# Column-wise norm roots spread by transposes, a tile-stepped first pair, and unrolled layers in a two-layer streaming encoder

## The chip, the cores and the metric

The kernel runs on one core of a Trainium2 chip. The metric is the device time of one launch in microseconds (us); lower is better. The engines are TensorE (PE, with its weight loads shown apart as PEld), VectorE (DVE), ScalarE (ACT), GpSimd (POOL) and SyncE (SP, which here issues the weight transfers).

## What is computed

Two layers run over 544 tokens at once: 512 prompt tokens (no history) and 32 later tokens with 256 cached ones. Each layer is a half-step gated feed-forward block, a mixer of three attention branches, and a second half-step feed-forward block. Each of these is a sandwich of two norms:

```
def rmsnorm(x, g):  return x * rsqrt(mean(x*x, axis=-1) + 1e-6) * g      # over 1024 features

def ffn_half(x, pre_g, w_up, w_down, post_g):
    h = rmsnorm(x, pre_g)
    gate, up = split(h  w_up, 2)                    # 1024 -> 2 * 2816
    y = (silu(gate) * up)  w_down                   # 2816 -> 1024
    return x + 0.5 * rmsnorm(y, post_g)

def mixer(x, ...):
    u = rmsnorm(x, mix_pre_gain)                     # then u  w_in, three attentions, gates, w_o
    return x + rmsnorm(y, mix_post_gain), new_rows

for l in range(2):
    x = ffn_half(x, ..0..);  x, new = mixer(x, ..);  x = ffn_half(x, ..1..)
```

The outputs are x after the second layer and the new cache rows of both layers.

## The kernel before, in words

**Layout.** Activations lie feature-major: `xT` is 128 partitions by 8 feature tiles by 544 tokens. A norm's sum over features is therefore a sum over partitions and over eight tiles. Products run in a split form: every weight tile is rounded to a high part by ACT (`high`, line 1030, into `piece_h` in the feed-forward blocks and `piece_m` in the mixer) and the rest is taken by POOL (`low`, line 398, back into the weight ring). Inputs are split in the same way, `uT_r` high and `u_l` or `u_lm` low. `split_product` (lines 584 to 602) does, for each of 8 feature tiles, high weight by high and by low input, in two token halves of 272 columns (4 matmuls at line 595), and then in a second sweep low weight by high input (2 at line 600): 48 matmuls for one 128-wide output tile. A feed-forward pair is a gate tile in PSUM unit 0 (banks 0 and 1) and an up tile in unit 1 (banks 2 and 3).

**Norms.** There are six wide norms in a layer: `pre_a`, `post_a`, `mix`, `mix_post`, `pre_b`, `post_b`. Before a sub-layer, ACT squares each new tile of `xT` into one of two `sq` buffers and `square_sum` (line 568) multiplies it by a 128x128 matrix of ones, two full fp32 matmuls of 272 columns for each of 8 tiles, so that the sum arrives in every partition of banks 4 and 5. After a sub-layer DVE adds seven squared tiles (line 1390) and `sum_partitions` (lines 578 and 581) does the same with two such matmul pairs. Then ACT takes the root of 128x544 (line 1009) and DVE the reciprocal (line 1364). `post_norm` scales tile k (line 1402) and adds tile k-1 to `xT` (line 1398). In a feed-forward block the input is split before its root is known (ACT line 1043, DVE line 1417) and the root is applied to the gate and up products (lines 1427 and 1429); the DVE splits stand behind the whole of `post_norm` in its queue. In the mixer the input is scaled first (line 1377) and then split (1025, 1374).

**Order at a boundary.** PE runs the eight square sums, then the gate tile of the first pair (its first sweep waits for tile k of the input at each k), then the up tile. The next gate tile needs unit 0 back from DVE (line 1427) and a new high piece from ACT.

**Loops.** Every engine has a hardware loop over the two layers (`Fori(0, DEPTH)`), with shorter ones within the feed-forward blocks. Semaphore targets are computed in registers from the loop variable. Gains of the layer are copied into `g_now` (lines 1649 and 1655).

**Start.** A table of position biases is made by PE and ACT (lines 538, 997) in the place where `act_h` will lie. POOL writes it to memory (line 382) and waits until it has landed (line 383) before its first `low`. DVE waits for the same before the first gated tile (line 1440).

## Time and profile before

| | us |
|---|---|
| median of 3 runs (3488.01 to 3491.17) | 3488.42 |
| the profiled execution | 3489.38 |
| its span, first to last instruction | 3487.8 |
| PE busy, share of the span | 3297.6, 95% |
| PEld busy | 2965.1, 85% |
| DVE, ACT, POOL busy | 1476.1, 1032.8, 1064.5 |
| share of the chain that ended last | PE 90%, DVE 5% |

The table is read from the top: PE sets the time in nearly all stages, so what is left lies in the stretches in which it waits or runs at a lower clock. These are the start of the kernel and the boundaries between sub-layers. PE's durations are modelled, and a busy PE is not one that streams at its peak: the share of a stretch in which columns stream has to be worked out from its instructions. The granted clock of a stretch is 1.0 at 2.4 GHz and 0.50 at 1.2 GHz.

### The profile page before, as it was taken

How to read it: one execution, taken by the hardware profiler on the slowest of the kernel's cores; microseconds unless marked ns; L12 is line 12 of the kernel's file. 1: busy time of each engine (PE TensorE's matmuls, PEld its weight loads, DVE VectorE, ACT ScalarE, POOL GpSimd, SP SyncE). 2: the span in 40 equal slices, each digit the busy share in tenths (PEclk: the TensorE clock that was granted, in tenths of full speed). 3: DMA queues.
4: the chain of work that ended last, by engine and by line, in shares of the span. 5: the costliest groups of instructions: out<-in, count | busy, mean ns of one | idle time of the engine just before them, and what ended most of it. 6: DMA issues, size and time to landing. Idle time of an engine off the chain costs nothing.

```text
span 3487.8 us, 57668 instructions
## 1 busy us (share of the span) xinstructions
PE 3297.6 (95%) x23070; PEld 2965.1 (85%) x23070; DVE 1476.1 (42%) x1874; ACT 1032.8 (30%) x1686; POOL 1064.5 (31%) x499
## 2 busy tenths in 40 slices
PE   3999989999999998999989999899999999899997
PEld 3999976966678898999989999779467779899997
DVE  1555141841235545554265531358202354365533
ACT  2222223243223323222232222332622232232221
POOL 1344322310213242334323443323011213334342
PEclk7999987998999999999999999889989999999999
DMA  5221232210111131221212212312011112312223
GB/s 128 85 84 70 91 112 77 77 41 10 61 37 58 55 114 64 94 84 65 105 69 90 84 67 98 107 65 85 9 50 39 46 50 72 115 61 90 83 73 118
DMA packets 43712, 259.99 MB, mean 75 GB/s; under 512 B 6112, under 2 KB 6208, under 8 KB 26112
## 3 DMA queue, kind: packets, MB, share of 16 engines
q1 hardware_dynamic: 37584, 239.83, 19.4%
q0 software_dynamic: 5840, 17.50, 1.9%
q8 instruction: 122, 2.00, 0.2%
q14 instruction: 70, 0.57, 0.1%
q10 hardware_dynamic: 96, 0.08, 0.0%
HBM read 241.54 MB, written 15.85 MB: 74 GB/s over the span
## 4 chain that ended last, share of the span: by engine, by line
PE 90%; DVE 5%; issue 2%; another core or an unknown queue 2%; ACT 1%; DMA 0%; DVEq 0%; POOL 0%; ACTq 0%; POOLq 0%
PE PS L595 38%; PE PS L600 19%; PE PS L784 11%; PE PS L945 2%; PE PS L556 2%; PE PS L683 2%; PE PS L704 2%; PE PS L896 1%; PE PS L898 1%; PE PS L795 1%; PE PS L568 1%; PE PS L809 1%; PE PS L825 1%; PE PS L812 1%
## 5 line engine op out<-in xcount | busy, mean ns | idle before, releaser
L398 POOL TENSOR_TENSOR ring_r<-ring,piece_h 128x1024 fp32r<-128x1024 f32 (+1 forms) x240 | 628.8, 2621 | 1066.0 <-ACT piece_h L1030 1010.7
L398 POOL TENSOR_TENSOR ring_r<-ring,piece_m 128x1024 fp32r<-128x1024 f32 (+1 forms) x172 | 365.8, 2131 | 1008.5 <-ACT piece_m L1030 1008.2
L595 PE MATMUL PS<-u_l,piece_h 128*128 128x272 f32 x2816 | 581.6, 288 | 0.0
L595 PE MATMUL PS<-uT_r,piece_h 128*128 128x272 f32 x2816 | 580.4, 287 | 0.6 <-DVE u_l L1417 0.6
L1030 ACT ACTIVATE piece_h<-ring 128x1024 fp32r<-128x1024 f32 (+1 forms) x240 | 275.0, 1147 | 1023.1 <-PE PS L600 1022.8
L600 PE MATMUL PS<-uT_r,ring_r 128*128 128x272 f32 x3648 | 497.1, 288 | 40.7 <-POOL ring_r L398 40.7
L600 PEld LDWEIGHTS PS<-uT_r,ring_r 128*128 128x128 f32 x3648 | 474.4, 189 | 40.9 <-POOL ring_r L398 40.9
L595 PEld LDWEIGHTS PS<-uT_r,piece_h 128*128 128x128 f32 x2816 | 441.0, 188 | 2.3 <-DVE u_l L1417 1.0
L595 PEld LDWEIGHTS PS<-u_l,piece_h 128*128 128x128 f32 x2816 | 440.4, 188 | 0.0
L595 PE MATMUL PS<-act_h,piece_h 128*128 128x272 f32 x1408 | 291.5, 288 | 0.0
L595 PE MATMUL PS<-act_l,piece_h 128*128 128x272 f32 x1408 | 291.4, 289 | 0.0
L1030 ACT ACTIVATE piece_m<-ring 128x1024 fp32r<-128x1024 f32 (+1 forms) x172 | 160.7, 936 | 368.4 <-PE PS L600 268.5
L1390 DVE TENSOR_TENSOR rstd<-rstd,sq 128x544 f32<-128x544 f32 x36 | 103.8, 2884 | 361.8 <-ACT sq L1002 361.8
L1429 DVE TENSOR_TENSOR sq<-sq,rstd 128x544 f32<-128x544 f32 x88 | 192.7, 2190 | 132.0 <-ACT sq L1048 132.0
L595 PEld LDWEIGHTS PS<-act_l,piece_h 128*128 128x128 f32 x1408 | 220.8, 188 | 0.0
L595 PEld LDWEIGHTS PS<-act_h,piece_h 128*128 128x128 f32 x1408 | 220.5, 189 | 0.0
L1437 DVE TENSOR_TENSOR act_l<-sq,act_h 128x544 f32 x88 | 211.3, 2401 | 10.8
L595 PE MATMUL PS<-uT_r,piece_m 128*128 128x272 f32 x832 | 180.2, 299 | 14.0 <-DVE u_lm L1374 13.3
L600 PE MATMUL PS<-act_h,ring_r 128*128 128x272 f32 x1408 | 186.2, 287 | 0.0
L600 PEld LDWEIGHTS PS<-act_h,ring_r 128*128 128x128 f32 x1408 | 179.9, 188 | 0.0
L595 PE MATMUL PS<-u_lm,piece_m 128*128 128x272 f32 x832 | 177.1, 295 | 0.0
L784 PE MATMUL PS<-uT_r,piece_m 128*128 128x272 f32 x768 | 163.8, 295 | 1.1 <-DVE xT L1524 1.1
(229 smaller groups left out, 4760.3 us busy)
## 6 DMA issues: line engine op xcount, KB each, us to landing
ring<-in_w_up SPq DMA_DIRECT2D x92, 1024.0 KB, 4.7
ring<-in_w_dn SPq DMA_DIRECT2D x64, 704.0 KB, 4.1
ring<-in_w_mg SPq DMA_DIRECT2D x48, 768.0 KB, 4.2
ring<-in_w_in SPq DMA_DIRECT2D x24, 1024.0 KB, 4.8
ring<-in_w_out SPq DMA_DIRECT2D x8, 1024.0 KB, 4.8
x_spill<-xT SPq DMA_DIRECT2D x2, 2176.0 KB, 8.7
xT<-x_spill SPq DMA_DIRECT2D x2, 2176.0 KB, 8.6
ring<-in_w_vb SPq DMA_DIRECT2D x4, 1024.0 KB, 4.7
```

The source lines that it names most:

```text
L398: nc.gpsimd.tensor_tensor(ring_r[:, ch[0] % NSLOT, at:at + n], w, hi, ALU.subtract).then_inc(S["w_low"], 1)
L556: ins = mm(PS[0:m, 2 * u + b, 0:n[b + 1] - n[b]], w, x[:, n[b]:n[b + 1]], start=first and s == 0, stop=last and s == len(steps) - 1)
L595: mm(PS[:, 2 * u + b, 0:HALF], w, x[k][:, HALF * b:HALF * b + HALF], start=first and k == 0 and n == 0, stop=False)
L600: ins = mm(PS[:, 2 * u + b, 0:HALF], w_l[:, k * P:(k + 1) * P], x_h[k][:, HALF * b:HALF * b + HALF], start=False, stop=last and k == K - 1)
L683: ins = mm(PS[:, banks[s], :], tokens(x, k, s), w[:, n], start=k == 0 and m == 0, stop=k == KD - 1 and m == 2)
L704: mm(PS[:, 6 + i % 2, 0:w], qI[r:r + 64, h // 2, P * s:P * s + P], kI[r:r + 64, k0:k0 + w], start=True, stop=True).then_inc(S["idx_done"], 1)
L784: ins = mm(PS[:, 2 * u + j % 2, 0:HALF], w, x[:, k, half], start=j < 2, stop=j >= 6 * K - 2)
L945: ins = mm(out, pt, V[0:m, vt, hv:hv + DH], start=n == 0, stop=n == len(tiles) - 1)
L1030: A(buf[:, hs, 0:n], ring[:, ch % NSLOT, at:at + n], ACT.Copy).then_inc(S["w_high"], 1)
L1390: ins = V.tensor_tensor(rstd[:], rstd[:], sq[:, k % 2, :], ALU.add) if k else V.tensor_copy(rstd[:], sq[:, 0, :])
L1429: V.tensor_tensor(g, g, rstd[:], ALU.mult).then_inc(S["gate_step"], 1)
L1437: V.tensor_tensor(lo, g, hi.bitcast(F32), ALU.subtract).then_inc(vacated[1], 1)
```

## The change

1. **Sums by token.** For the wide norms, `token_sums` replaces `square_sum`: the squared tile is the stationary operand, in five blocks of 128 tokens, and one column of ones streams past. The result is one column for each block, 128 tokens in the partitions. The root and the reciprocal are taken of 128x5 (`wide_root`, `finish`).
2. **Spread.** DVE multiplies a matrix of ones by each of the five columns (128x128 each), and PE transposes the five, so that every partition has the row of all tokens again, now in PSUM banks 4 and 5 (`r_tok`). The scaling of `post_norm` and of the mixer's input reads it there. A feed-forward block copies it to `rstd` first.
3. **Steps by tile.** Where a feed-forward block follows, `post_norm` on DVE goes scale, split, add for each tile instead of splitting all tiles at the end. On PE, `first_pair` runs gate and up tile together by feature tile: 8 matmuls for tile k, then (in feed-forward blocks) the token sums of tile k, then the 4 low-weight matmuls of tile k-3. ACT makes the high input before the square. The mixer's first two tiles go the same way after all its sums.
4. **Layers unrolled.** The loops over the layers are Python loops; targets are constants; `g_now` is gone. The four weight loads that followed the last block are gone.
5. **Table.** It lies at another address, and the wait for its landing moves on POOL to where it is read back; DVE's wait is gone. ACT loads the silu table set ahead of the loop.

```diff
+WIDE = {"pre_a": 0, "post_a": 1, "mix": 2, "mix_post": 3, "pre_b": 4, "post_b": 5}
+N_WIDE, N_TT = 6, 5
+TT_AT = [0, P, 2 * P, 3 * P, TOK - P]
+LAG = 3
-        topw_tab = region(0, NREL)
+        topw_tab = region(28288, NREL)
+        token_sum = PS[:, 6, 0:N_TT]
+        r_tok = unit(2).rearrange("p a b -> p (a b)")[:, 0:TOK]
...
# POOL
-            pool.wait_ge(S["table_out"], 16)
...
                 pool.wait_ge(S["qr_ready"], l * 2 + 2)
+                pool.wait_ge(S["table_out"], 16)
...
# PE
+            def token_sums(l, norm, k):
+                j, q0, K = NORMS[norm]
+                if k == 0:
+                    pe.wait_ge(S["root"], l * N_NORM + j + 1)
+                pe.wait_ge(S["sq_ready"], l * N_SQ + q0 + k + 1)
+                for t, at in enumerate(TT_AT):
+                    ins = mm(token_sum[:, t:t + 1], sq[:, k % 2, at:at + P], ones[:, 0:1], start=k == 0 and t == 0, stop=k == K - 1,
+                             skip_group_check=True)
+                ins.then_inc(S["sq_used"], 1)
+            def spread(l, norm):
+                for t in range(4):
+                    pe.wait_ge(S["spread"], (l * N_WIDE + WIDE[norm]) * N_TT + t + 1)
+                    nc.tensor.transpose(r_tok[:, P * t:P * t + P], spread_tile(t), ident)
+                pe.wait_ge(S["spread"], (l * N_WIDE + WIDE[norm]) * N_TT + N_TT)
+                mm(r_tok[:, SEQ:TOK], spread_tile(4)[P - NEW:P, :], ident[P - NEW:P, P - NEW:P], start=True,
+                   stop=True).then_inc(S["r_ready"], 1)
...
+            def first_pair(l, piece, w_l, x_h, x_l, h0, buf, after=None):
+                for k in range(KD + LAG):
+                    if k < KD:
+                        pe.wait_ge(S["hready"], l * 24 + h0 + k + 1)
+                        for g in range(2):
+                            if k == 0:
+                                pe.wait_ge(S["w_high"], piece + g + 1)
+                            for n, x in enumerate((x_h, x_l)):
+                                for b in range(2):
+                                    mm(PS[:, 2 * g + b, 0:HALF], buf[:, g, k * P:(k + 1) * P], x[k][:, HALF * b:HALF * b + HALF],
+                                       start=k == 0 and n == 0, stop=False)
+                        if after:
+                            after(k)
+                    if k >= LAG:
+                        q = k - LAG
+                        for g in range(2):
+                            if q == 0:
+                                pe.wait_ge(S["w_low"], piece + g + 1)
+                            for b in range(2):
+                                ins = mm(PS[:, 2 * g + b, 0:HALF], w_l[g][:, q * P:(q + 1) * P], x_h[q][:, HALF * b:HALF * b + HALF],
+                                         start=False, stop=q == KD - 1)
+                            if q == KD - 1:
+                                ins.then_inc(done[g], 1)
...
             def ffn(l, t0, c0, p0, pre, post, h0):
-                for k in range(KD):
-                    square_sum(l, pre, k)
...
-                up(0, c0, input_ready)
+                first_pair(l, l * PC_LAYER + p0, [...], u_h, u_lo, h0, piece_h, lambda k: token_sums(l, pre, k))
+                spread(l, pre)
...
# ACT
+            def wide_root(l, norm):
+                A(std_t[:], token_sum, ACT.Sqrt, scale=1.0 / (K * P), bias=eps_c[:]).then_inc(S["root"], 1)
...
# DVE
+            def finish(l, norm):
+                dve.wait_ge(S["root"], l * N_NORM + j + 2)
+                V.reciprocal(std_t[:], std_t[:]).then_inc(S["inv"], 1)
+                dve.wait_ge(S["inv"], l * N_NORM + j + 1)
+                alone(dve)
+                for t in range(N_TT):
+                    V.tensor_scalar(spread_tile(t), ones, std_t[:, t:t + 1], None, ALU.mult).then_inc(S["spread"], 1)
+                dve.wait_ge(S["r_ready"], l * N_WIDE + w + 1)
...
-                for k in range(KD):
-                    V.scalar_tensor_tensor(out=y[:, k, :], ..., in1=rstd[:], ...).then_inc(S["yscaled"], 1)
-                    if k:
-                        add(k - 1)
-                add(KD - 1)
+                scale(0)
+                scale(1)
+                add(0)
+                add(1)
+                if then:
+                    dve.wait_ge(S["xnew"], 8 + l * 24 + n_y * 8 + 1)
+                    then(0)
+                for k in range(2, KD):
+                    scale(k)
+                    if then:
+                        dve.wait_ge(S["xnew"], 8 + l * 24 + n_y * 8 + k)
+                        then(k - 1)
+                    add(k)
...
+                finish(l, pre)
+                V.tensor_copy(rstd[:], r_tok).then_inc(S["r_copied"], 1)
...
-            with dve.Fori(0, DEPTH) as l:
+            for l in range(DEPTH):
```

## Rows read from the trace of the kernel before

**Rows 1.** Waits of PE: total us, times, longest us.

```profile
PE PS L600 <- POOL ring_r L398: 40.7, 1, 40.7
```

**Rows 2.** Chain of the first 110 us: start us, us, what.

```profile
13.64 54.70 another core or an unknown queue
...
80.87 4.00 PE PS L595 x32
```

**Rows 3.** Timeline of layer 0's boundary `mix_post` to `pre_b`: start, us, instruction, idle.

```profile
1334.38 1.08 PE L578 MATMUL PS<-rstd,cst 128*128 128x272 f32 x4
...
1336.55 0.71 ACT L1009 ACTIVATE rstd<-PS,eps_c 128x544 f32<-128x544 f32 x1 [0.76 <-PE PS L581]
...
1337.30 3.55 DVE L1364 RECIPROCAL rstd<-rstd 128x544 f32<-128x544 f32 x1 [7.19 <-ACT rstd L1009]
1338.29 4.64 POOL L398 TENSOR_TENSOR ring_r<-ring,piece_h 128x1024 fp32r<-128x1024 f32 x2 [12.22 <-ACT piece_h L1030]
1340.88 3.32 DVE L1402 SCALAR_TENSOR_TENSOR arena<-arena,g_now,rstd 128x544 f32<-128x544 f32 x2
```

**Rows 4.** Chain where the second pair starts, layer 0 `pre_b`, layer 1 `pre_a`.

```profile
1368.77 3.25 PE PS L595 x26
...
1791.78 4.00 PE PS L595 x32
```

**Rows 5.** Timeline of the boundary between the layers, `post_b` to `pre_a`.

```profile
1753.45 1.08 PE L578 MATMUL PS<-rstd,cst 128*128 128x272 f32 x4
...
1761.27 1.28 ACT L1030 ACT_TABLE_LOAD   x1 [4.92 <-issue]
...
1776.87 0.19 DVE L1655 COPY g_now<-gain 128x45 f32 x1 [1.92 <-issue]
```

**Rows 6.** Windows: busy us of PE, PEld, DVE, ACT, POOL; clock; DMA; GB/s.

```profile
500.00:503.00 3.00, 2.89 (x11) 2.38 (x11) 2.66 (x7) 0.91 (x2) 0.00 (x0) 0.50 0.03 5
...
546.00:548.00 2.00, 2.00 (x6) 1.54 (x6) 0.00 (x0) 0.00 (x0) 0.00 (x0) 0.50 0.17 70
...
840.00:847.00 7.00, 6.92 (x46) 5.83 (x45) 0.00 (x0) 0.04 (x1) 0.00 (x0) 0.50 0.01 2
```

**Rows 7.** Timeline of PE in the same stage, two steps of the mixer's first tile.

```profile
497.59 0.82 PE L595 MATMUL PS<-uT_r,piece_m 128*128 128x272 f32 x2
...
498.92 0.82 PE L595 MATMUL PS<-uT_r,piece_m 128*128 128x272 f32 x2
```

**Rows 8.** PE groups of 16 to 18 us and of 20.6 to 23: busy us, mean ns.

```profile
L568 PE MATMUL PS<-sq,cst 128*128 128x272 f32 x4 | 2.2, 701 | 4.7 <-ACT sq L1002 4.7
...
L568 PE MATMUL PS<-sq,cst 128*128 128x272 f32 x9 | 2.6, 415 | 0.0
```

**Rows 9.** Weight loads by shape: of 495 to 503 us, and of the whole run.

```profile
L595 PEld LDWEIGHTS PS<-u_lm,piece_m 128*128 128x128 f32 x13 | 3.7, 330 | 0.0
...
L595 PEld LDWEIGHTS PS<-u_l,piece_h 128*128 128x128 f32 x2816 | 440.4, 188 | 0.0
```

**Rows 10.** Timeline of PE: thin fp32 matmuls at full clock and at half clock.

```profile
1147.05 0.78 PE L945 MATMUL PS<-arena 128*128 128x64 f32 x6
...
839.57 7.35 PE L872 MATMUL PS<-arena 128*64 128x32 f32 x48 [0.56 <-ACT arena L1277]
```

**Rows 11.** DVE groups by shape: busy us, mean ns, idle before.

```profile
L1429 DVE TENSOR_TENSOR sq<-sq,rstd 128x544 f32<-128x544 f32 x88 | 192.7, 2190 | 132.0 <-ACT sq L1048 132.0
...
L1427 DVE TENSOR_TENSOR sq<-PS,rstd 128x544 f32<-128x544 f32 x88 | 63.7, 724 | 210.8 <-PE PS L600 210.3 <-DVE rstd L1364 0.5
```

**Rows 12.** Timeline of PE after the mixer's seventh tile.

```profile
544.05 0.49 PE L683 MATMUL PS<-piece_m,uT_r 128*128 128x512 f32 x1 [1.93 <-ACT arena L1125]
```

**Rows 13.** Timeline of layer 0's boundary `post_a` to `mix`.

```profile
491.31 1.48 DVE L1377 SCALAR_TENSOR_TENSOR arena<-xT,g_now,rstd 128x544 f32<-128x544 f32 x2
...
511.95 0.41 PE L595 MATMUL PS<-uT_r,piece_m 128*128 128x272 f32 x2
```

**Rows 14.** Timeline of the last norm.

```profile
3470.02 1.48 DVE L1402 SCALAR_TENSOR_TENSOR arena<-arena,g_now,rstd 128x544 f32<-128x544 f32 x2
```

More of the change, by code:

```diff
@@ L407, in ffn @@
                     low(l, p0, 2 * KF + j, (c0 + KF + j, j % 2), 0, PIECE, piece_h)
-            with pool.Fori(0, DEPTH) as l:
+            for l in range(DEPTH):
                 ffn(l, PC_A, CH_A)
@@ L980, in attend @@
                     merge_span(l, m, 3, a, b)
-            with pe.Fori(0, DEPTH) as l:
+            for l in range(DEPTH):
                 ffn(l, T_A, CH_A, PC_A, "pre_a", "post_a", 0)
@@ L1333, in _ @@
             act.wait_ge(S["x_in"], 16)
-            with act.Fori(0, DEPTH) as l:
+            for l in range(DEPTH):
                 ffn(l, T_A, CH_A, "pre_a", "post_a", 0)
@@ L1381, in pre_norm, with split_input, post_norm @@
                 rest(KD - 1)
-            def post_norm(l, norm, y, half, n_y):
+            def split_input(l, pre, n_y, k):
+                dve.wait_ge(S["u_high"], (l * 3 + n_y) * KD + k + 1)
+                V.scalar_tensor_tensor(out=u_l[:, k, :], in0=xT[:, k, :], scalar=g_of(l, NORMS[pre][1] + k),
+                                       in1=uT_r[:, k, 0:TOK].bitcast(F32), op0=ALU.mult, op1=ALU.subtract).then_inc(S["hready"], 1)
+            def post_norm(l, norm, y, half, n_y, then=None):
                 c0 = NORMS[norm][1]
@@ L1513, in mixer @@
                     merge(l, m)
-                post_norm(l, "mix_post", y_m, False, 1)
+                post_norm(l, "mix_post", y_m, False, 1, lambda k: split_input(l, "pre_b", 2, k))
             def merge(l, m):
```

131 lines of the change are left out of this document (68 added, 63 removed).

## The prediction

> **What bounds the kernel now.** I read the time table first: PE is busy for 95% of the span, and the chain that ended last is 90% PE. DVE, ACT and POOL have slack on average, so a saving on them counts only where PE waits. The waits of PE then show one large hole, 40.7 us at the start, for POOL's first low piece [rows 1]. The chain of the first 110 us says why: from 13.64 for 54.70 us it runs through the write of the bias table, for which POOL waits before its first piece; the second gate-and-up pair starts at 80.87 [rows 2]. I call the start of the second pair the milestone of a boundary, since everything behind it runs at PE's own pace.
>
> The other holes are the boundaries. In the timeline of `mix_post` to `pre_b` the last product ends at about 1334.4; root and reciprocal are done at 1340.85, the first scaling takes until 1344.1 for two tiles [rows 3], and the second pair starts at 1368.77 [rows 4]: 34.4 us, of which the pair itself is 96 matmuls of 0.125 us (32 in 4.00 us [rows 4]), 12.0 us. The boundary between the layers is longer, 1753.4 to 1791.78, 38.4 us [rows 4, 5], also because ACT sits 4.92 us and DVE 1.92 us in the turn of the layer loop [rows 5].
>
> The third thing to see is PE's clock. In both boundary stretches it is at its lower level, 0.50, that is 1.2 GHz [rows 6]. At the start the granted clock reads 1.00, but the durations speak against it: the square sums' matmuls take 701 ns at 16 us and 415 ns after 20.6 us [rows 8], the same two levels as elsewhere. So PE enters the first pair at half clock there too.
>
> **The table's wait** (part 5). It goes. POOL's first piece can start when ACT has made the first high piece, at about 14.5 us, in place of 68.9. The table moves away from `act_h`, so DVE needs no wait; the wait on POOL before the read-back ends at 68.3 us, some 800 us before POOL gets there. Nothing is queued behind it that cares. What is late next is the input split: DVE's operands are both in SBUF, and such instructions are drawn out while POOL works. Of two groups of the same size and count, the one with both operands in SBUF has a mean of 2190 ns, the one that reads PSUM 724 [rows 11]; two scalings beside two POOL pieces took 3.32 us [rows 3]. Two low pieces from 14.5 to about 19.7 put the first split at 17.6 and the second at 20.6. PE starts at 17.6.
>
> **Root, reciprocal, spread** (parts 1, 2). Removed from the way of each wide norm: a root of 0.71 and a reciprocal of 3.55 us [rows 3]. Added: a root and a reciprocal of five columns (0.2 each, estimated from fixed costs; no row shows them), five writes of 128x128 and five transposes. A DVE pass of 544 columns takes 0.72 [rows 11], so one of 128 is at most 0.2; PE follows each at once. I put the five and the last transpose at 1.4 us, bounds 0.9 and 2.5. Net gain 2.0 us to 2.4 where it is on the path. In `post_norm` before a next block much of it is lost at once: the scaling now reads PSUM and passes POOL, but the adds have both operands in SBUF and meet the two low pieces of the next block, which ACT still hands over at the same time (POOL from 1338.3 for 4.64 us [rows 3]). One add fits between the two pieces and the next waits for the second. I get the first split tile at 1344.5, 10.1 us after the last product.
>
> **The token sums** (part 1) are the decisive term. Before, a tile's sum is 4 recorded matmuls of 272 columns. After, it is 5 fp32 matmuls, recorded as 10, each with a weight load of 128 columns of its own, and one column streamed. At full clock the nearest row is six matmuls with 128-column fp32 weights and 64 streamed columns in 0.78 us, less a last duration of 0.27: 0.10 to 0.11 us apiece [rows 10], so 1.1 us for a tile. At half clock the load itself is longer: 330 ns in place of 188 [rows 9]. The difference of 0.142 is more than the whole streaming time of one column, so I take a thin matmul at 0.215 us and a tile at 2.15. Bounds: 0.107 (the load does not slow the sequence) and 0.25. Another near row at half clock, 48 thin ones with half as many weight columns in 7.35 us, 0.153 each [rows 10], lies between.
>
> On this the Trainium skill differs from the trace. TensorE: Matmul & The Clock Gate, section LDWEIGHTS, gives the load time as the number of columns over 1.2 per ns, at either clock, which would be 107 ns for 128 columns; the trace's loads have 188 and 330 ns at the two clocks. By that figure a tile would be 1.07 us at half clock too, and the sum below would fall by 35 us.
>
> **Does the clock rise in the first pair?** [...] In 840 to 847 us PE is busy 6.92 of 7.00 us with thin matmuls and the clock stays at 0.50 [rows 6, 10]. In the mixer's first tile four matmuls stand in a step of 1.33 us (497.59 to 498.92 [rows 7]); at the half-clock rate of 0.25 that is at most 75% streaming, and the clock is still 0.50 in the whole of 500 to 503 [rows 6]. In a feed-forward first pair after the change, a step has 8 wide matmuls (k < 3) or 12, 2.0 or 3.0 us at half clock, beside 2.15 us of thin ones: 48% to 58% streaming. That is less than what did not lift the clock. I forecast that the whole first pair runs at 1.2 GHz in all four feed-forward blocks: 96 x 0.25 + 80 x 0.215 = 24.0 + 17.2 = 41.2 us. Before, the full-width square sums had lifted it ahead of the pair (701 ns, then 415 [rows 8]).
>
> **The turn into the second pair** (part 3). Before, the gate tile finished 6 us ahead of the up tile, and its way through DVE was covered by that. Now both finish together and the cover is gone. Queued on PE behind the pair are five transposes (1.1 at half clock), then DVE copies 544 columns (0.72) and makes the first gated product (0.72 [rows 11]) before unit 0 is free; with hops 2.9 us. ACT's new high piece runs beside it. Such a pause lets the clock fall: after a pause of 1.93 us [rows 12] it reads 0.50 in 546 to 548 [rows 6]. I add 1.5 us. Bounds for pause and re-warming together: 2.0 and 6.
>
> **Sum by boundary**, each to the milestone. `pre_b`: 10.1 + 41.2 + 4.4 = 55.7 against 34.4, +21.3, in two layers +42.6. `pre_a` of layer 1: 55.7 against 38.4, +17.3; the loop's turn, which unrolling takes away, is in this. Start: 17.6 + 41.2 + 4.4 = 63.2 against 80.9, -17.7. The four together: +42.2.
>
> `mix`, two times: the eight token sums stand alone at half clock, 2.15 a tile against DVE's step of 1.33, so PE is what is late: the last sum ends near 490.7 and the scaling starts at 492.5 in place of 491.31 [rows 13]. Then the pair of tiles is dense (12 wide matmuls in a step), the clock rises after about 5 us, and both tiles end near 509 in place of 511.95 [rows 13]. The pause behind them (high piece, then ACT's evacuation, 2.0 us, and part of a clock fall) takes the rest. I take 0, from -5 to +3 each.
>
> The last norm: scaling starts 2.0 us before 3470.02 [rows 14], and nothing else changes behind it: -2.0. Constants in place of register arithmetic in the mixer's short chains: -2.0, from 0 to -8. Code loading of the unrolled program, which no row shows: each layer's code is now run for the first time once, as layer 0's was before, so 0, at worst +5. The four loads after the end were on no path: 0.
>
> Total +42.2 - 2.0 - 2.0 = +38 against the profiled execution (span 3487.8, its own time 3489.38, 1 us above the median). On the median of 3488.4 that is 3526.
>
> **Rivals.** (a) The clock rises: the wide matmuls of a pair suffice to lift PE to 2.4 GHz after some 5 us, in spite of the thin ones. Then a pair takes 12.0 + 80 x 0.107 + 2.5 = 23.1 us, 18.1 less, four times 72, with a little less in the pauses: 38 - 74 = -36, 3452. This is the case that ends faster. [...] Against it speak rows 6, 7 and 10, for it that the pair follows upon work without gaps on PE, while the mixer's first tile had gaps. (b) The clock stays low but thin matmuls cost 0.107 at half clock: the pairs fall by 8.6 each and the mixer's sums keep pace, 38 - 34 - 7 = -3, 3485; the price of the pairs decides, and the row of 0.153 lets a middle case, about 3500, stand. (c) The change doesn't do what it says: DVE's interleaved steps are drawn out by POOL beyond the two pieces, so that PE waits in the pair; DVE's step is three passes, 2.1 us, below PE's 4 to 5, so this adds only if (a) holds, up to 10 us.
>
> **How the numbers follow.** Forecast 60%: 3526, by the bounds of its terms 3503 to 3542. (a) 23%: 3452, 3445 to 3470. (b) with the middle case 15%: 3480 to 3503. Others 2%. The range that leaves out no more than 2 in 10 must take in most of (a): 3448 to 3542. The likeliest case's own range is 3503 to 3542. A measurement of this kernel can tell about 0.2%, 7 us. Faster: (a) and a third of (b), 0.28. Same: the middle of (b), 0.07. Slower: 0.65.
>
> **What would show it.** In the profile after: the start of the second pair near 63 us in place of 80.9, and near 10.1 + 41 + 4 us after the last product at the later ones; granted clock 0.50 through the first pairs, thin matmuls 0.2 us apart there and 0.11 where the clock is full; PE busy longer by some 30 us in sum than before apart from the hole at the start. A granted clock of 1.00 in the middle of a first pair, or pairs of 25 us, would prove me wrong, and a first split tile much before or after 10 us would prove the lock between DVE and POOL misjudged.

## The result and the profile of the changed kernel

The changed kernel takes 3495.22 us (median of 17 runs, 3491.51 to 3507.53), the kernel before 3489.42 us (median of 17, 3486.63 to 3491.17): a ratio of 1.0025, with a 95% interval from 1.0018 to 1.0032. It is slower, as forecast, but by 6 us (0.25%) and not by 38. Its runs lie 16 us apart, those of the kernel before 4.5 us. The profiled execution of the changed kernel took 3502.37 us with a span of 3500.6, which is 7 us above its median; in spans it is 12.8 us slower than the kernel before. All line numbers below are those of the kernel named beside them. A wide matmul is one that streams 272 columns, a thin one streams a single column.

The start first. The hole of [rows 1] is gone from the waits of PE (engine, line, waited for: total us, times, longest us). What stands at the top now is the first split tile of the four pairs, and DVE's writes of the spread:

```profile
PE PS L650 <- DVE u_l L1468: 18.9, 4, 6.7
PE PS L591 <- DVE sq L1445: 13.6, 11, 1.8
```

The chain of the changed kernel's first 110 us answers to [rows 2] (start us, us, what):

```profile
49.29 1.81 PE PS L650 x8
51.10 1.93 PE PS L583 x10
53.03 3.43 PE PS L660 x16
59.20 5.80 PE PS L630 x32
```

L650 is the high part of a first pair, L660 its low part, L583 the thin matmuls of the token sums, L630 the next pair. Eight wide matmuls in 1.81 us and sixteen in 3.43 are PE at 1.2 GHz up to the end of the pair, and the second pair starts at 59.20 us in place of 80.87. Its first 32 matmuls take 5.80 us in place of 4.00: the clock is still low behind the pause.

The chain of the boundary `mix_post` to `pre_b` in layer 0 shows a pair in which the clock rises on the way:

```profile
1342.05 2.02 PE PS L650 x8
1344.08 1.93 PE PS L583 x10
1346.00 1.11 PE PS L660 x4
1347.12 1.81 PE PS L650 x8
1348.93 1.34 PE PS L583 x10
1350.27 0.60 PE PS L660 x4
1350.87 1.01 PE PS L650 x8
1351.88 1.01 PE PS L583 x10
...
1362.98 1.15 PE PS L630 x4
```

Up to 1348.9 each piece has the length of half clock, from 1350.3 on that of full clock. A tile's token sum costs 1.93 us before and 1.01 after. The granted clock says the same. These are windows of the changed kernel (busy us of PE, PEld, DVE, ACT, POOL, the granted clock, DMA share, GB/s): the two parts of this pair, and the token sums of the mixer's norm, which stand alone:

```profile
1331.00:1349.00 18.00, 18.00 (x84) 18.00 (x84) 11.40 (x17) 5.94 (x9) 0.00 (x0) 0.50 0.00 1
1349.00:1360.00 11.00, 11.00 (x91) 11.00 (x92) 2.05 (x7) 3.51 (x5) 0.00 (x0) 0.98 0.00 0
458.00:475.00 17.00, 16.97 (x80) 17.00 (x80) 8.32 (x12) 4.45 (x7) 4.16 (x7) 0.50 0.46 152
```

**Where the time went.** The table holds, for both profiled executions, the time from the end of the last product to the first matmul of the second pair (for the start: from the start of the span), and how far the changed kernel lies behind the other one at the end of the next product. That end comes after the slow first matmuls of the second pair, so it counts them too. In the two rows of `mix` it is taken at the start of the second pair, and the row below each carries the mixer behind it.

| stretch | before, us | after, us | length of the first pair after, us | behind after it, us |
|---|---|---|---|---|
| start | 80.87 | 59.20 | 38.8 | -19.6 |
| mix, layer 0 | 46.23 | 50.58 | 14.7 | -15.3 |
| the mixer of layer 0 | | | | -17.8 |
| pre_b, layer 0 | 34.07 | 46.25 | 30.2 | -3.7 |
| pre_a, layer 1 | 38.00 | 43.40 | 30.0 | +3.5 |
| mix, layer 1 | 46.24 | 47.75 | 14.3 | +5.0 |
| the mixer of layer 1 | | | | +2.6 |
| pre_b, layer 1 | 34.07 | 43.30 | 29.9 | +13.6 |
| the last norm | | | | +12.8 |

### The profile page after: what moved, and what is told of

It is laid out like the page before. It is cut to its first block, busy times and chain, and to the rows that moved or that the text cites. A ratio compares the mean times of both kernels' runs of the same rounds, so it can differ in the third digit from the quotient of the medians.

```text
span 3500.6 us, 55510 instructions
## 1 busy us (share of the span) xinstructions
PE 3362.7 (96%) x23502; PEld 3055.8 (87%) x23502; DVE 1341.5 (38%) x1933; ACT 975.7 (28%) x1647; POOL 1061.9 (30%) x499
## 4 chain that ended last, share of the span: by engine, by line
PE 93%; DVE 4%; issue 1%; ACT 1%; DMA 0%; DVEq 0%; SPq 0%; ACTq 0%
PE PS L630 37%; PE PS L635 18%; PE PS L846 11%; PE PS L583 2%; PE PS L1007 2%; PE PS L650 2%; PE PS L571 2%; PE PS L745 2%; PE PS L766 2%; PE PS L960 1%; PE PS L958 1%; PE PS L857 1%; PE PS L989 1%; PE PS L871 1%; PE PS L887 1%
## 5 line engine op out<-in xcount | busy, mean ns | idle before, releaser
L630 PE MATMUL PS<-uT_r,piece_h 128*128 128x272 f32 x2688 | 561.5, 291 | 7.9 <-DVE sq L1527 7.9
L630 PE MATMUL PS<-u_l,piece_h 128*128 128x272 f32 x2688 | 558.7, 289 | 0.0
L635 PE MATMUL PS<-uT_r,ring_r 128*128 128x272 f32 x3456 | 468.0, 288 | 0.0
L635 PEld LDWEIGHTS PS<-uT_r,ring_r 128*128 128x128 f32 x3456 | 446.4, 188 | 0.0
L630 PEld LDWEIGHTS PS<-uT_r,piece_h 128*128 128x128 f32 x2688 | 424.3, 190 | 8.3 <-issue 8.3
L630 PEld LDWEIGHTS PS<-u_l,piece_h 128*128 128x128 f32 x2688 | 424.7, 190 | 0.0
L630 PE MATMUL PS<-act_l,piece_h 128*128 128x272 f32 x1408 | 292.2, 290 | 0.0
L630 PE MATMUL PS<-act_h,piece_h 128*128 128x272 f32 x1408 | 291.4, 288 | 0.0
L630 PEld LDWEIGHTS PS<-act_h,piece_h 128*128 128x128 f32 x1408 | 220.8, 189 | 0.0
L630 PEld LDWEIGHTS PS<-act_l,piece_h 128*128 128x128 f32 x1408 | 220.6, 188 | 0.0
L1537 DVE TENSOR_TENSOR act_l<-sq,act_h 128x544 f32 x88 | 214.5, 2437 | 10.8
L1534 DVE TENSOR_TENSOR act_h<-sq,PS 128x544 f32 x88 | 63.5, 722 | 321.0 <-PE PS L635 320.5
L846 PE MATMUL PS<-uT_r,piece_m 128*128 128x272 f32 x768 | 164.4, 295 | 0.9 <-DVE xT L1618 0.9
L630 PE MATMUL PS<-uT_r,piece_m 128*128 128x272 f32 x768 | 162.0, 292 | 3.1 <-ACT arena L1181 3.1
L630 PE MATMUL PS<-u_lm,piece_m 128*128 128x272 f32 x768 | 159.8, 289 | 0.0
```

Of the source, the lines that this page charges most:

```text
L630: mm(PS[:, 2 * u + b, 0:HALF], w, x[k][:, HALF * b:HALF * b + HALF], start=first and k == 0 and n == 0, stop=False)
L635: ins = mm(PS[:, 2 * u + b, 0:HALF], w_l[:, k * P:(k + 1) * P], x_h[k][:, HALF * b:HALF * b + HALF], start=False, stop=last and k == K - 1)
L846: ins = mm(PS[:, 2 * u + j % 2, 0:HALF], w, x[:, k, half], start=j < 2, stop=j >= 6 * K - 2)
L1537: V.tensor_tensor(lo, g, hi.bitcast(F32), ALU.subtract).then_inc(vacated[1], 1)
```

## The experiments

The kernel before ran beside each group of these kernels, with medians from 3488.46 to 3489.33 us, so times of different groups can be compared to about 1 us.

### The table alone

The first kernel is the kernel before with the table's part of the change.

```diff
-        topw_tab = region(0, NREL)
+        topw_tab = region(28288, NREL)
@@ POOL, ahead of its first piece
-            pool.wait_ge(S["table_out"], 16)
@@ POOL, ahead of the read-back in the mixer
+                pool.wait_ge(S["table_out"], 16)
@@ DVE, ffn
-                if n_y == 0:
-                    dve.wait_ge(S["table_out"], 16)
```

> The kernel before with the table's part of the change alone (table moved off act_h, POOL's wait put ahead of the read-back, DVE's wait gone). My sum priced that part only together with the new order: in it the start went from 80.87 to 63.2. Theory of the account after the result: the first pair now ends in the old order at its old pace, so the whole 40.7 us hole goes but for what POOL's pieces still need: low piece 1 is ready at about 17.5, the square sums of the first tiles end near 30.6, and PE runs on. The second pair starts near 41 to 44 us in place of 80.87, and the kernel takes 3488 - 37 = 3451 (3446 to 3456). Then the rest of the change costs 40 to 45 us in the median, not the 12 that the comparison of the two kernels shows. Rival: the hole was only covering something that is late anyway (weights of the next chunks landing by DMA, or DVE's split beside POOL), and less than 25 us come back: 3463 or more.

It takes 3445.36 us (3444.66 to 3446.02; ratio 0.9875, 0.9859 to 0.9890). The chain of its start (start us, us, what; L568 is the full-width square sum, L595 and L600 the pairs):

```profile
16.14 5.58 PE PS L568 x16
21.73 0.00 issue
21.73 1.18 PE PS L568 x4
...
38.49 4.00 PE PS L595 x32
```

The second pair starts at 38.49 us, 42.4 earlier than before and 20.7 earlier than in the changed kernel. The other boundaries are what they were (34.06 and 37.97 us where the kernel before has 34.07 and 38.00). So this part is worth -44, and the rest of the change costs +50. The rival falls; the second pair started earlier than the 41 to 44 us that I expected, and the time is just under the range.

### The layers unrolled as well

The loops over the two layers become Python loops, and nothing else changes.

```diff
-            with pe.Fori(0, DEPTH) as l:
+            for l in range(DEPTH):
@@ and so on all five engines, on top of the table's part
```

> The kernel before with the table's part (3445.4 by itself) and the layers unrolled on all five engines; norms, order and sums as before. Theory: the turn of the layer loop goes (ACT sat 4.92 us in it, DVE 1.92; about 4 us of the path) and the short chains of the mixer lose register arithmetic (in the kernel after each mixer was 2.1 and 2.5 us shorter): 3445.4 - 4 - 4.6 = 3437 (3434 to 3441). Rival: code of the second layer that is fetched for the first time costs what the turn gives back, and the mixer's gain in the kernel after came from something else: 3443 or more.

It takes 3437.06 us (3435.20 to 3438.59; ratio 0.9851, 0.9834 to 0.9867). Of the 8 us between the two profiled executions the boundary between the layers gives 3.7 (37.97 us to 34.31), the mixers give 0.5 and 2.2, and the other boundaries most of the rest. Unrolling is worth -8, as expected, with no cost to be seen for the second layer's code. What is left of the change, the norms and the order, costs 3495.2 - 3437.1 = 58 us.

### Fewer thin matmuls

In the norms ahead of the feed-forward blocks, feature tiles 1 to 7 are summed over the first 128 tokens alone. The kernel so leaves out 56 of the 80 thin matmuls of a pair, and with them most of the sum.

```diff
-                for t, at in enumerate(TT_AT):
+                for t, at in enumerate(TT_AT if k == 0 or norm == "mix" else TT_AT[:1]):
                     ins = mm(token_sum[:, t:t + 1], sq[:, k % 2, at:at + P], ones[:, 0:1], ...
```

> The kernel after; in the norms ahead of the feed-forward blocks the token sums of feature tiles 1 to 7 are taken over the first 128 tokens only (1 of 5 thin fp32 matmuls, 2 recorded in place of 10), so most of the sum is left out; all else stays. Theory A (the thin matmuls' own time, and the low clock that they hold): a pair has 96 wide and 24 thin in place of 80. With 8 wide matmuls and 2 thin ones in a step PE is held by DVE's three passes (about 2.3 us a step), and the clock rises some 10 us into each pair, in the start pair too: pairs of 20 to 22 us in place of 30.0 (three) and 38.8 (start, to about 25). Kernel 3495 - 3*9 - 13 = 3455 (3448 to 3463). Theory B (thin matmuls cost their time, 56 * 0.1 us at either clock, and the clock in these stretches follows from the pause ahead): 3495 - 4*6 = 3471 (3466 to 3480), with the clock low for as long as now.

It takes 3450.22 us (3448.70 to 3450.54). The four pairs, from the start to layer 1's `pre_b`, take 18.5, 19.2, 19.3 and 19.1 us. The chain through the first of the `pre_b` pairs:

```profile
1315.63 2.02 PE PS L650 x8
1317.65 0.22 PE PS L583 x2
1317.87 1.49 PE PS L650 x8
1319.36 0.12 PE PS L583 x2
1319.47 0.61 PE PS L660 x4
1320.08 1.00 PE PS L650 x8
```

Here the clock rises at about 1318.5, some 9 us into the pair, in the changed kernel 19 us in. A later pair is 10.8 us shorter. Of this the 56 thin matmuls left out are 5.7 us even at full clock (56 times 0.101), and the rest is time that was run at 1.2 GHz. Theory A holds, and its pairs came out still shorter than it asked.

### Keeping PE busy ahead of the pair

Matmuls whose result nobody reads fill PE's pauses between the last product and the pair.

```diff
+            def keep_busy(n):
+                for _ in range(n):
+                    mm(PS[:, 7, 0:256], ones, cst[:, 0:2, :].rearrange("p a b -> p (a b)"), start=True, stop=True)
@@ spread
+                    if t and norm in ("mix_post", "post_b"):
+                        keep_busy(1)
@@ ffn
+                keep_busy(6 if l == 0 and h0 == 0 else 8)
```

> The kernel after with matmuls without use (ones by a constant of 256 columns, to a PSUM bank that is free there) that keep PE busy over the pause ahead of each first pair: one before each of the 3 transposes of the norm ahead, 8 behind it, 6 at the start. All results stay. Theory A (the low clock of the pair comes from the pauses of 1.8, 1.8 and 4.1 us ahead of it and then lasts because the pair streams too little): the pair begins at 2.4 GHz; if thin matmuls mixed with wide ones do not let it fall, each later pair takes 20 to 21 us in place of 30.0 and the kernel 3495 - 3*9 = 3468, less up to 14 at the start (3452 to 3470). Theory B (the mix of thin and wide itself lets the clock fall, wherever it stood): the pair runs at 1.2 GHz again after some microseconds, gains 0 to 4 us each, and the kernel takes 3485 to 3497.

It takes 3491.36 us in the median of 10 runs, but these run from 3472.95 to 3506.14, the widest spread of all kernels here. In the profiled one the four pairs took 31.2, 26.1, 35.4 and 30.8 us. Two windows of the third, which begins at 1749.10 with the clock up:

```profile
1749.20:1763.80 14.60, 14.60 (x84) 14.60 (x83) 11.61 (x18) 6.42 (x10) 0.00 (x0) 0.64 0.00 1
1764.00:1784.50 20.50, 20.50 (x97) 20.50 (x96) 2.46 (x8) 3.61 (x6) 0.00 (x0) 0.51 0.00 0
```

PE has no pause in either window, and the clock still goes down and stays down. The other two later pairs also begin at 1.00 and are at 0.50 some 5 us in; it comes back after 14 us in one and after 24 in the other. So theory A falls: the pair is at the low clock without a pause ahead of it. The median fits theory B, but two of the ten executions took 3473 and 3475 us, which no trace explains. In the kernels with all the thin sums in the pair, the mix lets the clock fall from above, and from below lets it rise late or not at all.

### The same pair, dense

The token sums in the pair are replaced by the full-width sums of before, at the same place, with the full-width root and reciprocal behind.

```diff
-                           piece_h, lambda k: token_sums(l, pre, k))
-                spread(l, pre)
+                           piece_h, lambda k: square_sum(l, pre, k))
@@ ACT
-                wide_root(l, pre)
+                root(l, pre)
@@ DVE
-                finish(l, pre)
-                V.tensor_copy(rstd[:], r_tok).then_inc(S["r_copied"], 1)
+                invert(l, pre)
```

> The kernel after; the norms ahead of the feed-forward blocks take their sum as before (all-ones weights, the squares of a tile streamed in full width, to two banks of their own), at the same place inside the first pair, with the full-width root and reciprocal behind it. Theory A (streaming share holds the clock): the pair is now dense in streaming; at half clock a step has 8 or 12 wide matmuls and a sum of about 1.8 us, so the clock rises within some 10 us, in the start pair too, and then DVE's three passes (2.3 us a step) pace it: pairs of 20 to 23 us in place of 30.0 and 30 to 39. The root of 0.71 and the reciprocal of 3.55 take the place of the short finish, with no up tile to cover them: +3 each. Net three times -6, the start about -12: 3495 - 30 = 3465 (3455 to 3475). Theory B (the thin matmuls are dear only by their count, the clock has another cause): the pair stays 28 us or more and the kernel comes to 3495 to 3510.

It takes 3459.22 us (3458.16 to 3460.79; ratio 0.9916, 0.9899 to 0.9932), 36 less than the changed kernel and inside theory A's range. The four pairs take 21.9, 21.9, 22.0 and 21.9 us. Chain of the same boundary (L651 high part, L604 full-width sum, L661 low part):

```profile
1307.49 2.15 PE PS L651 x8
1309.64 1.81 PE PS L604 x4
1311.45 1.50 PE PS L651 x8
1312.96 0.92 PE PS L604 x4
...
1328.16 3.56 DVE rstd L1433
```

The clock is up 5 us into the pair. The rows also give the price of the two kinds of sum: four wide matmuls take 0.92 us at full clock and 1.81 at half, ten thin ones 1.01 and 1.93. **The thin sums are not cheaper at either clock.** What they save is behind the pair: there this kernel has a root of 0.72 and a reciprocal of 3.56 us, and the second pair starts 3.5 us after the pair's end where it is 2.7 in the changed kernel.

So the thin sums of these norms are worth 36 of the 58 us. The other 22 (3459.2 against 3437.1) stand between this kernel and the one with the table and the unrolled layers. By their profiled executions 18 of them arise at the four pairs: the second pair starts 42.8, 36.1, 36.2 and 36.1 us after the last product (or the start of the span) in place of 38.7, 33.8, 34.3 and 33.7, and behind it come low first matmuls. **The new order by feature tile costs time even when its pair is dense.** Which of its parts does so was not taken apart; the turn into the second pair, which the old order covered by the up tile, is the likely one.

### Low parts from the first step on

The low-weight matmuls of tile k follow at once and not three steps later.

```diff
-LAG = 3
+LAG = 0
```

> The kernel after with LAG = 0: each step of a first pair has 12 wide matmuls and the token sum from the first on, in place of 8 for three steps, 12 for five and 4 for the last three. The work is the same; only the streaming share of the first steps is higher (3.0 of 5.0 us at half clock in place of 2.0 of 3.9). Theory A (share decides; in the kernel after the clock rose only once the 12-step part had begun, some 19 us into the pair): it rises some 10 us into the pair, and each later pair takes about 25 us in place of 30.0: 3495 - 3*5 = 3480 (3474 to 3488), the start about 2 us later since the low pieces are needed at once. Theory B (the clock in these pairs rises after a fixed time from its fall, whatever the share): pairs of 29 to 31 us as before and 3493 to 3500.

It takes 3492.32 us (median of 10, 3488.24 to 3498.49). The four pairs take 24.3 us at the start, then 26.9, 28.9 and 26.7. The pairs lie between the theories, and the time is just under the range of theory B. The clock rises 12, 16 and 12 us into the later pairs where it took 18 to 20. Each later pair is 1 to 3 us shorter and the start's is far shorter, but the pause behind the pair grows from 2.7 us to between 3.6 and 4.2, and the total moves by 3 us, less than these runs scatter.

### Thin sums in the old order

For this and the last kernel a version was made of the parts that paid: table, unrolled layers, the short finish in the norms behind a block, the mixer's two input tiles by feature tile; the norm's sums in the mixer and ahead of the feed-forward blocks as before, and there the old order too. By itself it was the following run.

> A version made from the parts that paid: table, unrolled layers, short roots with spread by transposes in the norms behind a block alone (post_a, mix_post, post_b), the two input tiles of the mixer by feature tile, but its norm with full-width sums; the norms ahead of the feed-forward blocks, the order of their input (residual first, split behind) and the first gate tile ahead of the up tile all as before. By theory A the wide sums lift the clock ahead of the pair again. From e8's expected 3437: short finish -2.0 to -3.5 in each of five places behind a block, less what the lock beside POOL takes back (in the kernel after the writes took 3.2 to 5.3 us in place of 1.07): -5 in all; the last one -1; the mixer's pair -2 each: 3437 - 10 = 3427 (3421 to 3434). Rival: the lock takes all of it, and the version is level with e8.

It takes 3430.81 us (3423.89 to 3431.40; ratio 0.9827, 0.9811 to 0.9844). Its boundaries are 32.8, 32.4 and 32.8 us, and 43.4 in the mixer in place of 46.2. It is 6 us faster than the kernel with the table and the unrolled layers, within the range expected, so the rival falls.

Upon it one thing is changed back:

```diff
-                    square_sum(l, pre, k)
+                    token_sums(l, pre, k)
@@ up, between the gate and the up tile of the first pair
+                        if step and g:
+                            spread(l, pre)
@@ ACT
-                root(l, pre)
+                wide_root(l, pre)
@@ DVE
-                invert(l, pre)
+                finish(l, pre)
```

> e9 (3430.8) with one thing changed: the norms ahead of the feed-forward blocks take their sums again by thin matmuls (token sums, short finish, spread between the gate and the up tile), all eight ahead of the pair and not mixed with it. Theory A (thin matmuls alone hold PE at 1.2 GHz and cost 0.2 us each there, so 2.0 us a tile against the 1.45 that DVE's step allows): the sums end 5 us later at each boundary and the pair starts at the low clock and loses some 4 us more: 3431 + 4*8 = 3463 (3452 to 3470), and since the pair then is dense, the times of single runs stay within 4 us of each other. Rival (the order by feature tile and the mixing with the pair is what costs, thin sums ahead of the pair do not): 3440 or less.

It takes 3469.20 us (3468.34 to 3470.11; ratio 0.9943, 0.9928 to 0.9958): +38.4 for the thin sums with their short root and spread, within the range expected, and the boundaries are 42.4, 42.0 and 42.4 us, 9.6 more each. Its chain at `mix_post` to `pre_b`:

```profile
1309.68 17.20 PE PS L584 x80
1326.87 6.76 PE PS L633 x32
1333.63 1.38 PE PS L638 x11
```

Eighty thin matmuls take 17.20 us, 0.215 each. In the kernel with full-width sums this stretch is

```profile
1297.56 7.77 PE PS L604 x20
1305.33 0.00 issue
1305.33 1.18 PE PS L604 x4
...
1308.88 4.01 PE PS L633 x32
```

11.3 us long, since DVE's step sets its pace, and the pair behind it starts at full clock (32 matmuls in 4.01 us, not 6.76). Both halves of theory A are here: 5.9 us in the sums and 2.8 in the first 32 matmuls. The runs of this kernel lie 1.8 us apart, as expected of one whose pair is not mixed. The rival, that only the mixing costs, falls.

### The changed kernel once more

Nothing is changed here; it is a second profiled execution of the changed kernel.

> The kernel after once more, unchanged, for a second profile. Its times lie between 3491 and 3508, those of the kernels whose pairs are dense within 4 us. Theory: the mix of thin and wide in a first pair sits near what lifts the clock, so the same pair is at times 30 and at times 39 us long. In the profile at hand the four pairs took 38.8, 30.2, 30.0 and 29.9 us; in this one at least one of the four differs by over 2 us from its value there, and the difference of the two spans is that of the pairs within 2 us. Rival: the pairs agree within 1 us, and the spread of the times lies elsewhere (DMA landings, POOL).

It took 3499.21 us, with a span of 3497.4. The pairs took 34.3, 30.0, 29.8 and 29.8 us: three as before, the one of the start 4.5 us shorter. Its chain there:

```profile
41.23 1.93 PE PS L583 x10
43.16 1.11 PE PS L660 x4
44.27 1.76 PE PS L650 x8
46.04 1.01 PE PS L583 x10
```

The clock rises at about 46 us, which in the other profiled execution it never did before the pair ended. In the kernel of the next experiment, whose PE program is the same, that pair took 30.2 us. So one and the same stretch of PE work takes 30, 34 or 39 us. The spans differ by 3.2 us and the four pairs by 5.0 in sum, within the 2 us that I had allowed. The rival falls, though not all of the scatter lies in the pairs: from the mixer's second pair of tiles to its last product layer 0 took 822.7 us here and 820.1 in the other execution. Of the 20 such stretches in the profiled executions of the changed kernel and the versions made from it, four are some 3 us longer than the one in the same execution's other layer. What causes it is open.

### The writes of the spread read PSUM

The prediction had noted that DVE instructions with both operands in SBUF are drawn out beside POOL. Here one operand of the five writes lies in PSUM.

```diff
-                    V.tensor_scalar(spread_tile(t), ones, std_t[:, t:t + 1], None, ALU.mult)
+                    V.tensor_scalar(spread_tile(t), token_sum[:, 0:1].broadcast_to([P, P]), 0.0, std_t[:, t:t + 1], ALU.mult, ALU.add)
```

> The kernel after, where the five 128x128 writes that spread the roots read a PSUM column (times zero, plus the root) in place of the ones in SBUF. Theory: these writes took 5.07 us (449.29), 5.27 (1319.84), 3.17 (1752.64) beside POOL's two low pieces and 1.07 alone (475.85), because both operands were in SBUF; with the operand in PSUM they take 1.1 to 1.5 us everywhere. What follows in post_a and pre_b: the scalings read PSUM and pass POOL, but the residual's add has both operands in SBUF and meets POOL next, so of the 2 to 4 us won in each of the four stretches about half comes through: -4 to -9 in all, 3486 to 3491. Rival: the writes are as slow as before, since it is writing to SBUF that collides: within 1 us of the kernel after.

It takes 3492.16 us (median of 11, 3487.86 to 3498.98), 3 less than the changed kernel, whose own runs lie 16 us apart. That is outside both forecasts, 4 to 9 less and within 1. In the changed kernel the writes and POOL's pieces stand so at `post_a` in layer 0 (timeline: start, us, instruction):

```profile
449.29 5.07 DVE L1445 TENSOR_SCALAR sq<-cst,std_t 128x128 f32<-128x128 f32 x4 [0.17 <-issue]
449.53 4.74 POOL L412 TENSOR_TENSOR ring_r<-ring,piece_m 128x1024 fp32r<-128x1024 f32 x2 [15.30 <-ACT piece_m L1098]
```

With the operand in PSUM, at the boundary between the layers:

```profile
1737.23 1.39 DVE L1445 TENSOR_SCALAR sq<-PS,std_t 128x128 f32<-128x128 f32 x5
...
1737.92 4.65 POOL L412 TENSOR_TENSOR ring_r<-ring,piece_h 128x1024 fp32r<-128x1024 f32 x2 [15.30 <-ACT piece_h L1098]
...
1740.88 2.91 DVE L1490 SCALAR_TENSOR_TENSOR xT<-arena,xT 128x544 f32<-128x544 f32 x2
```

The writes pass beside POOL (all 60 of them took 340 to 353 ns), and what is hit is the next instruction with both operands in SBUF, the residual's add: 2.91 us for two in place of 1.35. The first split matmul comes 10.6 to 10.8 us after the last product, where it was 13.4 once and 10.7 twice. At `post_a` of layer 0, where two writes had been hit as well, the mixer's sums let the pair begin 32.1 us after the last product in place of 34.3. So only where two writes had been hit does anything come through.

### A version that beats both

```diff
@@ mixer, on top of the version with the old order ahead of the feed-forward blocks
+                for _ in range(12):
+                    mm(PS[:, 4, 0:256], ones, cst[:, 0:2, :].rearrange("p a b -> p (a b)"), start=True, stop=True)
@@ DVE, finish: the writes read PSUM, as above
```

> e9 (3430.8) with two additions: the spread's writes read PSUM (as in e4), and 12 matmuls without use (256 columns, to a bank that is free there) keep PE busy through the root and reciprocal of the mixer's norm, 7.2 us, ahead of a pair that is dense and ran at half clock for its first 10 us. Theory: now that wide matmuls follow, a clock that is up stays up: the mixer's two input tiles end about 3 us earlier in each layer, and the writes give 0 to 3 us in all: 3423 (3418 to 3428). Rival: the pair waits for DVE's step of 1.45 us anyway (8 wide matmuls at 1.0 us a step), the clock falls in it, and the version is level with e9.

It takes 3425.02 us (3423.05 to 3430.70; ratio 0.9820, 0.9807 to 0.9833). The two windows hold the same 96 matmuls, the mixer's first two tiles, in this kernel and, under it, in the version without the matmuls of no use. The granted clock is the third figure from the right:

```profile
450.50:463.40 12.90, 12.78 (x96) 12.07 (x96) 8.76 (x16) 4.11 (x7) 0.00 (x0) 1.00 0.25 100
```

```profile
450.60:465.50 14.90, 14.90 (x96) 14.78 (x96) 8.83 (x16) 4.06 (x7) 0.00 (x0) 0.79 0.22 87
450.50:455.00 4.50, 4.44 (x19) 4.47 (x20) 4.50 (x8) 1.98 (x3) 0.00 (x0) 0.50 0.75 295
```

The third line is the first part of the second window: without the added matmuls the pair begins at 0.50. The mixer boundary is 41.4 us in place of 43.4, in both layers, and the time is within the range expected. The pair itself is still held by DVE's step for its first half, so the gain is 2 us a layer and not 3. The single runs of the two versions overlap, so the 6 us between their medians are less sure than the 2 us at each of the two boundaries.

## Why the prediction was right in sign and wrong in size

In the terms of the prediction's sum, for the profiled executions (the low first matmuls of the second pair counted with their boundary, as there):

| term | forecast, us | measured, us |
|---|---|---|
| start | -17.7 | -19.6 |
| `pre_b`, layers 0 and 1 | +21.3 and +21.3 | +14.0 and +11.0 |
| `pre_a`, layer 1 | +17.3 | +7.2 |
| `mix`, layers 0 and 1 | 0 and 0 | +4.4 and +1.5 |
| shorter chains of the mixer | -2.0 | -4.9 |
| last norm | -2.0 | -0.8 |
| sum | +38 | +12.8 |

**The step that failed** is the one on the clock: "I forecast that the whole first pair runs at 1.2 GHz in all four feed-forward blocks: [...] 41.2 us." The pairs took 38.8, 30.2, 30.0 and 29.9 us, together 36 us less. (The sum came out only 25 us lower, since writes beside POOL and the `mix` boundaries took some of it back.) Only the start's pair ran at 1.2 GHz to its end, and that only in this execution. In the other three the clock rose 19 to 20 us in. What misled me was the use of [rows 6, 7]: in 500 to 503 us of the kernel before, the mixer's first tile runs at 0.50 with at most 75% streaming, and I concluded that a pair that streams less stays low to its end. The last experiment shows another cause for a low clock of this kind. With PE kept busy through the root and reciprocal ahead of it, a pair with the same wide matmuls, paced by the same step of DVE, has a granted clock of 1.00. There it was the pause ahead that held the clock low at first. This is shown for the order by feature tile; the kernel before's own order was not tried so. The second row that I leaned on was right: the clock does stay low under thin matmuls alone (80 in 17.20 us).

**The sign** was right by a small margin, a gain of 20 us at the start against losses of 32 behind it. And the time lies in the range that I gave to rival (b) and its middle case, 3480 to 3503, by luck: that case asked for cheap thin matmuls at a low clock, and they were neither cheap nor always at the low clock.

**Rival (a)** had the clock rise after 5 us "in spite of the thin ones". That is what the dense pair does (5 us), not the mixed one. The truth lay between forecast and rival: the mixed pair sits where the clock rises late and not each time. Neither the forecast nor the rival had a term for that, and it explains much of the spread of the runs: between the three profiled executions with pairs of 38.8, 34.3 and 30.2 us at the start the spans are 3500.6, 3497.4 and 3488.5. (Some 6 us of the last are due to the faster writes of that kernel.) The runs of the four kernels whose first pair is mixed with all the thin sums spread over 10 to 33 us (10 to 17 runs each), those of the seven others over 1.4 to 7.7 (4 or 5 runs each, which makes a small spread likelier), and those of the kernel before over 4.5 (17 runs). Rival (c), DVE late inside the pair, did not come up: PE is busy for all of its windows there.

**Price of a thin matmul.** 0.215 at half clock was right where they stand alone (17.20 us for 80), and in the pair it is 0.193 (1.93 for ten); at full clock it is 0.101, as forecast. So rival (b) falls. That these sums are the largest term of the loss is shown twice: by the two kernels in the old order that differ in them, +38.4 us, and by the two in the new order, +36. The Trainium skill (TensorE: Matmul & The Clock Gate, section LDWEIGHTS) gives one formula for the load, by which 128 columns take 107 ns, and names no clock beside it. Thin matmuls that follow each other at 0.101 us agree with that at full clock; at half clock they take nearly the double, and the recorded loads are longer at both, 188 and 330 ns [rows 9].

**First split tile.** Forecast 10.1 us after the last product, measured 10.7 twice and 13.4 once. I let the wait for POOL hit the adds, and it hit the five small writes ahead of them, which I had put at 1.4 us, transpose included, with 2.5 as the upper bound. They took 3.2 to 5.3, for one or two of the five each took 2.37 us, the length of one of POOL's instructions. Alone one took 0.28, where I had said at most 0.2. At `post_a` of layer 0 the five took 5.5 us in the same way. The root and the reciprocal of five columns, which no row had shown, took 0.27 and 0.19 us where I had estimated 0.2 each.

**The turn into the second pair** was right: 2.7 us from the pair's end to the next one, transposes included, and 1.8 of low clock, 4.5 in place of 4.4.

**`mix`.** The eight sums took the 17.2 us of the forecast, with PE late behind DVE. But they ended 29.1 and 26.8 us after the last product where the forecast had 25.0, and the scaling began at 31.8 and 29.5 where it had 26.8. From there to the end of the two tiles it was 17.2 and 16.7 us, near the forecast's 16.5. From -5 to +3 was the range. Layer 0 fell outside it by the two writes that waited for POOL.

**The table** (part 5) went as told. The second pair began at 59.20; the forecast's 63.2 has 1.5 us of low clock in it that comes after this point, and the rest of the difference is the pair, 38.8 us in place of 41.2. But I priced it only inside the sum of the start, and so did not see how large a gain stood by itself: 44 us, of which the new order gave 21 back at the start alone.

**Unrolling and constants.** The mixers are 4.9 us shorter where I had put 2.0, but not all of it is due to unrolling: 2.8 us of it stand in layer 0 already in the kernel that moves the table alone (819.8 us from the second pair of tiles to the last product in place of 822.6), and such a stretch varies by 3 us between executions. Unrolling by itself gave 0.5 and 2.2 there. **The last norm** gave 0.8: the scaling now reads PSUM, and a step of scaling and add is 1.45 us in place of 1.33, which takes back nearly 1 us over eight tiles.

## What to carry to other kernels

Price the parts of a change one at a time: here one part was worth -44 us, another -8, and the rest +58, and the sum of the three said nothing of any. Before wide matmuls are replaced by thin ones, compare both in PE's own time (here 0.92 us against 1.01) and ask what the clock does under them, since a stretch that PE fills without a gap can still run at 1.2 GHz. When the single runs of a kernel suddenly spread by more than those of its neighbour, profile it twice and compare the stretches. Here one held a stretch in which the clock rose at a different time in each execution, and while it was there, differences of 3 us between variants could not be told.

## What the runs showed of the hardware that I had not expected

The same PE program took 38.8, 34.3 and 30.2 us for the same 176 matmuls in three profiled executions, without a pause in any: the clock rose in the middle, near the end, or not at all.

PE that enters a mixed stretch with its clock up can lose it there without a single pause (a granted clock of 0.51 over 20.5 us in which PE was busy for 20.5).

At the start of the span the granted clock does not fit the durations. In the changed kernel it says 1.00 for a stretch in which eight wide matmuls take 1.81 to 2.02 us, the lengths of 0.50 elsewhere:

```profile
18.00:56.00 38.00, 38.00 (x174) 38.00 (x174) 8.15 (x13) 10.36 (x15) 1.68 (x1) 1.00 0.54 88
```

A DVE write of 128 by 128 elements with both operands in SBUF takes 0.28 us alone and up to 2.38 beside a POOL instruction of 2.37 us; the same write with its operand in PSUM takes 0.34 to 0.35 us everywhere, and the wait moves on to the next instruction with both operands in SBUF (two adds in 2.91 us in place of 1.35).
